# Activation parts laid out in two halves of 128 columns, 256 bytes apart modulo 512

## What is computed

```
def _swiglu(h, w_in, w_out):
    gate, up = jnp.split(h @ w_in, 2, axis=-1)
    return (jax.nn.silu(gate) * up) @ w_out
# first block: 2 layers, each
x = x + 0.5 * _swiglu(_rmsnorm(x, g[0]), ffn_w_in[li, 0], ffn_w_out[li, 0])
x = x + mixer(_rmsnorm(x, g[1]))            # gated linear attention, then latent attention
x = x + 0.5 * _swiglu(_rmsnorm(x, g[2]), ffn_w_in[li, 1], ffn_w_out[li, 1])
x = x + sigmoid(_rmsnorm(x, g[3]) @ ple_w_gate[li]) * (p[li] @ ple_w_in[li])
# second block: 2 layers, each
h = rmsnorm(x, g_pre[l]) * (1.0 + scale) + shift
x = x + gate * rmsnorm(hybrid_mixer(h, w_in[l], w_out[l], ...), g_post[l])
```

## Time and profile before

| | us |
|---|---|
| median of three runs | 1520.99 |
| the profiled execution | 1515.71 |
| its span, first to last instruction | 1513.9 |
| PE (matmul) busy | 1470.3 (97%) |
| DVE busy | 1085.6 (72%) |
| ACT busy | 765.3 (51%) |
| mean granted TensorE clock | 0.994 of 2.4 GHz |

### The profile page before, as it was taken

The page is one execution under the profiler, slowest core; times in us unless marked ns, Lnnn a source line. Parts: engine busy times, 40 slices in busy tenths (PEclk is TensorE's granted clock), DMA queues, the critical chain, the costliest instruction groups (busy, mean ns, idle before and its releaser), DMA issues.

```text
span 1513.9 us, 31080 instructions
## 1 busy us (share of the span) xinstructions
PE 1470.3 (97%) x12390; PEld 1416.5 (94%) x12390; DVE 1085.6 (72%) x1573; ACT 765.3 (51%) x1154; POOL 170.5 (11%) x218
## 2 busy tenths in 40 slices
PE   6999999999999999999999999999998999999998
PEld 6999999989999999999999889999998997889968
DVE  5887568987897568876667655797668667485582
ACT  5554455565554457544444355454346437454382
POOL 1111012711230110100010000110110100010000
PEclk9999999999999999999999999999999999999999
DMA  6887744226786755776655225787653853047400
GB/s 208 257 267 228 258 141 157 90 79 208 235 273 225 226 153 178 256 226 224 198 162 146 84 84 168 234 275 236 208 173 117 233 144 111 1 136 228 143 1 29
DMA packets 219069, 264.86 MB, mean 175 GB/s; under 512 B 22270, under 2 KB 196318, under 8 KB 218974
## 3 DMA queue, kind: packets, MB, share of 16 engines
q1 hardware_dynamic: 209000, 234.64, 49.7%
q0 software_dynamic: 8960, 27.37, 5.4%
q10 hardware_dynamic: 1013, 1.52, 0.3%
HBM read 262.44 MB, written 1.05 MB: 174 GB/s over the span
## 4 chain that ended last, share of the span: by engine, by line
PE 83%; DVE 9%; ACT 4%; DMA 2%; issue 1%; DVEq 0%; POOL 0%; SPq 0%; ACTq 0%
PE twin L1124 24%; PE twin L1126 24%; PE twin L1125 24%; DVE w_lo L1875 3%; PE twin L1369 1%; PE twin L1553 1%; PE twin L1793 1%; PE twin L1755 1%; ACT w_hi L700 1%; DVE rs L1904 1%; PE twin L1567 1%; PE twin L1565 1%; DMA w_raw<-in_ffn_w_in 1%; PE twin L1138 1%; PE twin L1204 1%
## 5 line engine op out<-in xcount | busy, mean ns | idle before, releaser
L700 ACT ACTIVATE w_hi<-w_raw 128x1024 fp32r<-128x1024 f32 (+1 forms) x452 | 454.9, 1038 | 425.9 <-PE twin L1126 263.7
L1124 PE MATMUL twin<-xh,w_lo 128*128 128x256 f32 x2312 | 651.9, 282 | 11.8 <-DVE w_lo L1875 7.4
L1875 DVE TENSOR_TENSOR w_lo<-w_raw,w_hi 128x1024 fp32r<-128x1024 f32 (+1 forms) x452 | 547.7, 1248 | 146.1 <-ACT w_hi L700 144.8
L1125 PE MATMUL twin<-xl,w_hi 128*128 128x256 f32 x2312 | 645.4, 279 | 0.0
L1126 PE MATMUL twin<-xh,w_hi 128*128 128x256 f32 x2312 | 645.2, 279 | 0.0
L1124 PEld LDWEIGHTS twin<-xh,w_lo 128*128 128x128 f32 x2312 | 436.8, 189 | 16.5 <-issue 7.3
L1125 PEld LDWEIGHTS twin<-xl,w_hi 128*128 128x128 f32 x2312 | 437.8, 189 | 1.6 <-issue 1.2
L1126 PEld LDWEIGHTS twin<-xh,w_hi 128*128 128x128 f32 x2312 | 436.2, 189 | 0.2
L1124 PE MATMUL twin<-hh,w_lo 128*128 (+1 forms) x704 | 194.6, 276 | 0.0
L1125 PE MATMUL twin<-hl,w_hi 128*128 (+1 forms) x704 | 194.3, 276 | 0.0
L1126 PE MATMUL twin<-hh,w_hi 128*128 (+1 forms) x704 | 194.3, 276 | 0.0
(11 more groups left out here) (382 smaller groups left out, 1989.3 us busy)
## 6 DMA issues: line engine op xcount, KB each, us to landing
w_raw<-in_ffn_w_in SPq DMA_DIRECT2D x176, 512.0 KB, 4.8
w_raw<-in_ffn_w_out SPq DMA_DIRECT2D x88, 512.0 KB, 4.2
w_raw<-in_w_in SPq DMA_DIRECT2D x52, 512.0 KB, 4.8
mod_raw<-in_w_ada POOLq DMA_DIRECT2D x128, 192.0 KB, 4.4
w_raw<-in_a_w_in SPq DMA_DIRECT2D x32, 512.0 KB, 4.3
w_raw<-in_ple_w_gate SPq DMA_DIRECT2D x16, 512.0 KB, 4.4
w_raw<-in_b_w_out SPq DMA_DIRECT2D x16, 512.0 KB, 3.7
w_raw<-in_w_out SPq DMA_DIRECT2D x16, 512.0 KB, 4.5
```

The lines of the kernel that those rows point to most:

```text
L700: A(w_hi[:, c % NSLOT, cols], w_raw[:, c % NRAW, cols], ACT.Copy).then_inc(*did(hi_ready))
L1124: mm(out, lhs[1], rhs[0], start=start, stop=False, skip_group_check=skip)
L1125: mm(out, lhs[0], rhs[1], start=False, stop=False, skip_group_check=skip)
L1875: V.tensor_tensor(w_lo[:, c % NSLOT, cols], w_raw[:, c % NRAW, cols], f32(w_hi[:, c % NSLOT, cols]), ALU.subtract).then_inc(*did(lo_ready))
```

## The change

The tiles `xh`, `xl`, `hh`, `hl` get the shape (partition, half, tile x 128 + 64): all first halves (tokens 0 to 127) of all tiles, then 256 bytes of gap, then all second halves. The first half of each tile begins 64 bytes past a multiple of 512 from `w_at`, the second half 320 bytes past one (for `xh` the halves are 1088 x 4 = 4352 = 8 x 512 + 256 bytes apart). A moving operand is then two runs of 512 bytes instead of one of 1024, and the matmul, the ScalarE and the VectorE instructions that read or write these tiles name both runs; no instruction is added or left out. In the token-wise chunks the stationary tile is still one run, at 64 for the first tokens and at 320 for the second. `LINEAR_STEP` keeps `region`, and so `oh`, `cqh`, `hg_oh` and `pth`, at 448. PSUM is written as before.

```
-OPERAND_STEP = 448
+LINEAR_STEP = 448
+SPLIT_STEP = 64
+GAP = 64
...
-    base[0] += (OPERAND_STEP - (base[0] - w_at)) % 512
-    xh = fixed("xh", [P, KD, T], F32R)
-    xl = fixed("xl", [P, KD, T], F32R)
-    region = base[0]
+    base[0] += (SPLIT_STEP - (base[0] - w_at)) % 512
+    xh = fixed("xh", [P, 2, KD * P + GAP], F32R)
+    xl = fixed("xl", [P, 2, KD * P + GAP], F32R)
+    region = base[0] - GAP * 4
+    region += (LINEAR_STEP - (region - w_at)) % 512
...
-    place, _ = at_offset(region)
-    hh = place("hh", [P, KF, T], F32R)
-    hl = place("hl", [P, KF, T], F32R)
+    place, pos = at_offset(region)
+    pos[0] += (SPLIT_STEP - LINEAR_STEP) % 512
+    hh = place("hh", [P, 2, KF * P + GAP], F32R)
+    hl = place("hl", [P, 2, KF * P + GAP], F32R)
+    pos[0] -= GAP * 4
...
-    place, _ = at_offset(region + 2 * KF * T * 4)
+    place, _ = at_offset(region + 2 * KF * T * 4 + 1024)
...
+    def tiles(a, k, n=1):
+        return a[:, :, k * P:(k + n) * P]
+    def columns_of(a, k):
+        return tiles(a, k) if a.shape[2] > T else two(a[:, k, :])
+    def tokens_of(a, k, t):
+        return a[:, t, k * P:(k + 1) * P] if a.shape[2] > T else a[:, k, t * P:(t + 1) * P]
+    def pairs(ap):
+        return ap.rearrange("p a (h n) -> p h a n", h=2)
...
-                A(xh[:, k, :], X[:, k, :], ACT.Copy, scale=gain(k)).then_inc(*did(act_steps, ("xh", nu, k)))
+                A(columns_of(xh, k), two(X[:, k, :]), ACT.Copy, scale=gain(k)).then_inc(*did(act_steps, ("xh", nu, k)))
...
-                A(hh[:, k, :], hid_t[:, p % 2, :, :], ACT.Copy).then_inc(*did(hidden_hi))
+                A(hh[:, :, k].rearrange("p h (a n) -> p h a n", a=2), pairs(hid_t[:, p % 2, :, :]), ACT.Copy).then_inc(*did(hidden_hi))
...
+            if len(rhs[0].shape) == 3 and len(out.shape) == 2:
+                out = two(out)
             mm(out, lhs[1], rhs[0], start=start, stop=False, skip_group_check=skip)
...
-                                 [a[:, k, :] for a in xs], k == 0, k == KD - 1)
+                                 [columns_of(a, k) for a in xs], k == 0, k == KD - 1)
...
-                        kk = 2 * q + k if it is None else bass.ds(2 * q + k + 8 * it, 1)
-                        xk = [a[:, kk, :] if it is None else a[:, kk, :].rearrange("p a n -> p (a n)") for a in (hh, hl)]
+                        kk = (2 * q + k) * P
+                        kk = slice(kk, kk + P) if it is None else bass.ds(kk + 8 * P * it, P)
+                        xk = [a[:, :, kk] for a in (hh, hl)]
```

More of the change, by code:

```diff
@@ L768, in first_pair @@
                 act.wait_ge(hidden_ready, n0 + 1)
-                A(hh[:, 0:2, :], hid_t[:, 0, :, :], ACT.Copy).then_inc(*did(hidden_hi))
+                A(tiles(hh, 0, 2).rearrange("p h (a n) -> p h a n", a=2), pairs(hid_t[:, 0, :, :]), ACT.Copy).then_inc(*did(hidden_hi))
             first_pair()
@@ L1031, in _ @@
                 act.wait_ge(*when(("xn", l, k)))
-                A(xh[:, k, :], sq[:, k, :], ACT.Identity, bias=mods[:, l, k:k + 1]).then_inc(*did(act_steps, ("xh", nu, k)))
+                A(tiles(xh, k), two(sq[:, k, :]), ACT.Identity, bias=mods[:, l, k:k + 1]).then_inc(*did(act_steps, ("xh", nu, k)))
             c0 = first[f"win{l}"]
@@ L1069, in y_hi @@
                     act.wait_ge(*when(("y", l, k)))
-                    A(xh[:, k, :], yC[:, k % 2, :], ACT.Copy).then_inc(*did(act_steps, ("yh", l, k)))
+                    A(tiles(xh, k), two(yC[:, k % 2, :]), ACT.Copy).then_inc(*did(act_steps, ("yh", l, k)))
             for i, (kind, m, start, stop) in enumerate(ITEMS):
@@ L1163, in as_they_come @@
                     last = three(bank[b][:, n * T:(n + 1) * T], [a[:, k, n * P:(n + 1) * P] for a in w],
-                                 [a[:, k, :] for a in xs], k == 0 and n == 0, k == KD - 1, True)
+                                 [columns_of(a, k) for a in xs], k == 0 and n == 0, k == KD - 1, True)
             return last
@@ L1181, in columns @@
                         last = three(bank[b][:, n * T:(n + 1) * T], [a[:, k, n * P:(n + 1) * P] for a in w],
-                                     [a[:, k, :] for a in xs], k == 0, k == kd - 1)
+                                     [columns_of(a, k) for a in xs], k == 0, k == kd - 1)
             last.then_inc(*did(pe_groups, name))
@@ L1682, in project @@
                     for k in range(KD):
-                        last = three(bank[b][0:24, 0:T], [a[:, k, :] for a in w], [a[:, k, :] for a in xs], k == 0, k == KD - 1)
+                        last = three(bank[b][0:24, 0:T], [a[:, k, :] for a in w], [columns_of(a, k) for a in xs], k == 0, k == KD - 1)
                     last.then_inc(*did(pe_groups, key))
@@ L1811, in wout @@
                         last = three(bank[j][:, i * T:(i + 1) * T], [a[:, k, i * P:(i + 1) * P] for a in w],
-                                     [a[:, k, :] for a in xs], k == 0 and i == 0, k == KD - 1, True)
+                                     [columns_of(a, k) for a in xs], k == 0 and i == 0, k == KD - 1, True)
                     if k == KD - 1:
@@ L1880, in low @@
                 dve.wait_ge(*when(("xh", nu, k)))
-                V.scalar_tensor_tensor(xl[:, k, :], X[:, k, :], gain(k), f32(xh[:, k, :]), ALU.mult, ALU.subtract).then_inc(*did(dve_steps, ("xl", nu, k)))
+                V.scalar_tensor_tensor(columns_of(xl, k), two(X[:, k, :]), gain(k), f32(columns_of(xh, k)), ALU.mult, ALU.subtract).then_inc(*did(dve_steps, ("xl", nu, k)))
         def norm(nu, gain, late=(), add=None):
@@ L2396, in _ @@
                 dve.wait_ge(*when(("xh", nu, k)))
-                V.scalar_tensor_tensor(xl[:, k, :], sq[:, k, :], mods[:, l, k:k + 1], f32(xh[:, k, :]), ALU.add, ALU.subtract).then_inc(*did(dve_steps, ("xl", nu, k)))
+                V.scalar_tensor_tensor(tiles(xl, k), two(sq[:, k, :]), mods[:, l, k:k + 1], f32(tiles(xh, k)), ALU.add, ALU.subtract).then_inc(*did(dve_steps, ("xl", nu, k)))
             lo(c0 + 1)
@@ L2537, in gated_lo @@
                     dve.wait_ge(*when(("yh", l, k)))
-                    V.tensor_tensor(xl[:, k, :], yC[:, k % 2, :], f32(xh[:, k, :]), ALU.subtract).then_inc(*did(dve_steps, ("yl", l, k)))
+                    V.tensor_tensor(tiles(xl, k), two(yC[:, k % 2, :]), f32(tiles(xh, k)), ALU.subtract).then_inc(*did(dve_steps, ("yl", l, k)))
             maxima_c(0)
```

9 lines of the change are left out of this document (5 added, 4 removed).

## The result

The changed kernel took 1529.2 us (median of 10 runs, 1524.1 to 1535.11) against 1521.45 us for the kernel before on the same chip (10 runs, 1517.07 to 1524.14): a ratio of 1.0056 [1.0037, 1.0075], slower by 7.75 us. The profiled execution took 1532.15 us, with a span of 1530.3 us, 16.4 more than before.

A forecast was written before the change was run, and what follows sets the result against it. TensorE, 97% busy, was taken to bound the kernel through its matmuls' distances. Terms of -11, 0, 0 and 0 us took the profiled 1515.71 to 1504.7; with medians 5.3 us higher, the forecast was 1509.5 us, range 1489 to 1533.

The forecast's parts named there:

- (a): Matmuls on `xh`, `xl`, `hh`, `hl`: 2,500 slow ones would become fast, 4.4 ns each, worth 11 us.
- the picture of one read overtaking the other modulo 512: In TensorE, moving and stationary reads hinder each other at equal offsets modulo 512; halves at 64 and 320 would avoid overtaking.
- The step from the profiled execution to the median: The median of the runs stands 5.3 us above the profiled execution; the forecast carried this over to the changed kernel.
- (d): Token-wise chunks, 480 matmuls, with new stationary offsets, and the tiles' writers: taken as 0, bounds +0.9 and -1.2 us.
- (b): Fast rhythm of the 9,048 matmuls: might shorten from 113.3 to 111.7 ns, worth 15 us; taken as 0.
- Rivals 1a and 1b: Matmul distance falls everywhere: to the load's 111.7 ns, 1495 us, chance 0.19; or to 110 ns or less, 1476, 0.07.
- (c): A second run in the moving pattern of the 9,048 matmuls: bounded at -1 and +2 ns each, taken as 0.
- Rival 4: A second run in the moving pattern costs 1 to 2 ns a matmul: 1519 to 1539 us, chance 0.11.
- Rival 2: Offsets change nothing; how TensorE starts sets the rhythm and the mix is drawn anew: 1521 us, within 4, chance 0.17.
- Rival 3: The slow rhythm takes over through the start at 64 or the jump: 6,500 fast matmuls slow, +29 us, 1550, chance 0.14.
- its case with half of the 9,048 slow: The milder outcome of the slow rhythm taking over, with half of the matmuls slow: 1529 us.

The follow-up runs named there:

- grids 1 and 2: Two kernels of matmul streams without the blocks' computation, varying operand offsets, runs and jumps, the second also weights moved by 64 bytes: 893.5 and 1117.7 us.
- e4_half448: The changed kernel with its halves at 448 and 192 modulo 512: 1515.07 us, ratio 1.0003 to the kernel before.
- e2_lin64: The kernel before with OPERAND_STEP = 64, one run 64 bytes past a multiple of 512, tiles behind `region` moved too: 1532.2 us, ratio 1.0104.
- the four grids: Four kernels of 36-matmul streams without the blocks' computation, measuring the rhythm alone for different operand layouts: 893.5, 1117.7, 1124.4 and 1122.4 us.
- e10_lo128: The kernel before with `w_lo` 128 bytes further on: 1505.32 us, ratio 0.9916 to the kernel before.
- e3_same448: The changed kernel with GAP = 0 and SPLIT_STEP = 448, two runs both at 448 modulo 512: 1514.99 us, ratio 1.0005 to the kernel before.
- same64: A stream layout, not a full kernel: moving operand in two runs that both begin at 64 modulo 512; fast in 4 of 10 streams.
- grid 3: A kernel of matmul streams without the blocks' computation, moving tile in two runs from and to various places: 1124.4 us, no layout under 113.3 ns.
- grid 2: A kernel of matmul streams without the blocks' computation, with places between the 64s, other jumps, weights moved by 64 bytes, and mid-stream place switches: 1117.7 us.

## Why the prediction was wrong

**(a) The slow rhythm goes, -11 us.** This is the step that failed, in its sign. What held: the operands' distance bears on the rhythm, the two rhythms are 113.3 and 117.8 ns, and 2,500 slow matmuls was a good reading (2,565 counted). What did not: the picture of one read overtaking the other modulo 512. The period is 256 (grids 1 and 2), so what I took for a layout without an overtaking, 64 and 320, is a tile at place 64 in one piece; `e4_half448`, the same jump from the old place, changed nothing. The change comes down to moving the operands from 192 to 64, and 192 was the one place of the eight tried where one-run tiles took the fast rhythm in the grids. The same loss comes from one constant in the kernel before (`e2_lin64`). Measured for the term: +20.8 us in place of -11, from the two traces. By the medians the whole change is worth +7.75 us, where -11.5 was forecast. The step from the profiled execution to the median (+5.3 us) did not carry over either: the changed kernel's median lies 3 us below its profiled execution.

The warning was in my own rows. The token-wise chunks at 64 the other way had both rhythms, `ckh` at 128 was slow, and I used the second for "the place matters" and put the first down under (d) with a bound of 1 us. Both say that no place other than the present one was known to be better, and the picture was not tried against the earlier trace rows: it could have given the slow rhythm at 64 as well as the fast one.

**(b) The floor stays: 0.** Right. No stream or long stretch that ran, in the 63 layouts of the four grids and in `e10_lo128` with 8,714 fast matmuls, went under 113.3 ns. Rivals 1a and 1b fall. The Trainium skill, "TensorE: Matmul & The Clock Gate", section "Back-to-back issue gap", would have 109.2 ns; no run here shows it for float32r with a new stationary tile for each matmul.

**(c) Two runs: 0.** Right: `e3_same448` is 1.0005 [0.9986, 1.0024], which bounds it at 1.0024 x 1515 less 1515 = 3.6 us on 9,048 matmuls, 0.4 ns, as far as the mix of rhythms was the same. Rival 4 falls. **(d) Token-wise chunks, and the writers: 0.** Near enough: the 480 matmuls take 57.8 us after 56.3. Modulo 256 their place went from 64 to 192, and 83 fewer are slow, but 16 more ran at the lower clock, which the bounds did not have. ACT and DVE are as busy as before, and PE waits no longer for them.

**Rival 2** (nothing) had a true part: how TensorE starts sets the rhythm at place 192, and the mix is drawn anew. But the place decides which rhythms can be drawn. **Rival 3** is what happened, and I had given it 0.14. Its sign in the profile, a mean above 276 ns on `hh` and `hl`, is there. Its size in the traces was 4,680 of the 6,500 matmuls, 21 us of its 29; longer distances gave 9.0 us back. The reason is one of the two that rival gave, the start at 64 and not the jump. But that the time, 1529.2, lies in the range and on the 1529 of its case with half of the 9,048 slow is luck: 7,245 were slow, for which its sum gives about 1542.

**Open.** What in a start at place 192 makes it fast or slow: neither the length of the stall nor the work ahead of it sorted the streams. Why the full kernel has fast stretches at 64, and two runs at the same place 64 fast streams (`same64`). And what stands behind the distance modulo 256: that the two reads of TensorE meet somewhere is my guess, and two models of it failed in grid 3.

## What to carry to other kernels

When TensorE is bound by back-to-back float32r matmuls with a new stationary tile each, lay out moving and stationary tiles with the difference of their byte offsets in view: by its value modulo 256 a matmul cost 113.3 to 120 ns here, and in the whole kernel the worst place cost 3.1% more than the present one. Read the rhythm from windows (matmuls in 100 us) and not from busy shares, which are 97% at either; and before a layout is changed for a picture, run the one constant that separates the parts of the change: a short kernel of streams showed in one run that the place was wrong and the jump was nothing. Here one line that moves `w_lo` by 128 bytes gives 0.9916 [0.9893, 0.9939].

## What the runs showed of the hardware

- The distance of float32r matmuls (128 x 128 stationary, 256 moving columns) at 2.4 GHz depended on the moving tile's offset less the stationary one's, modulo 256 (grids 1 and 2, one run): 120.0 ns at 0, 116.7 at 32, 117.8 at 64, 120.0 at 96, 118.7 at 128 (120.0 in 4 of 20 streams), 117.3 or 118.7 at 160, 113.3 or 117.8 at 192, 118.5 at 224. Two runs that both begin at 64 were fast in 4 of 10 streams, and the full kernel at 64 had a fast stretch of over 1,000 matmuls, so this is not the whole rule. At 1.2 GHz the distance was 213 ns in every kernel.
- At 192 the same code and addresses run in either of two rhythms, and a stretch keeps its own, for over 1,000 matmuls in the kernel before; a switch to place 64 ends it within a matmul (grid 2).
- With `w_lo` moved by 128 bytes the slow rhythm at 192 is no longer kept: a stream leaves it within 12 matmuls, and 8,714 of some 9,000 matmuls of the full kernel are fast.
- A moving operand in two runs of 512 bytes, both at place 448, costs what one of 1024 costs: 1.0005 [0.9986, 1.0024] in the full kernel, 0.4 ns a matmul at most if the mix of rhythms was the same.
